# A transformer layer in split fp32: three seven-product units in each up block of the second feed-forward, and longer splits on VectorE

## What is computed

```python
h = rmsnorm(x, ffn2_norm[l])
x = x + 0.5 * swiglu(h, ffn2_w_gate[l], ffn2_w_up[l], ffn2_w_down[l])
...
def swiglu(h, w_gate, w_up, w_down):
    return (jax.nn.silu(h @ w_gate) * (h @ w_up)) @ w_down
```

## Time and profile before

| | |
|---|---|
| median of 3 runs | 1926.8 us (1924.58 to 1927.35) |
| the profiled execution, its own time | 1926.48 us |
| its span, first to last instruction | 1924.7 us |
| granted clock of TensorE | 1.000 |
| PE busy | 1914.1 us (99%), 8998 matmuls |
| DVE busy | 1247.9 us (65%), 1460 instructions |
| ACT busy | 971.4 us (50%), 1232 instructions |
| DMA | 362.51 MB, mean 188 GB/s |
| the blocks (second feed-forward) | from about 1274 us to the end |

### The profile page before, as it was taken

The page is one execution under the profiler, slowest core; times in us unless marked ns, Lnnn a source line. Parts: engine busy times, 40 slices in busy tenths (PEclk is TensorE's granted clock), DMA queues, the critical chain, the costliest instruction groups (busy, mean ns, idle before and its releaser), DMA issues.

```text
span 1924.7 us, 22367 instructions
## 1 busy us (share of the span) xinstructions
PE 1914.1 (99%) x8998; PEld 1608.3 (84%) x8998; DVE 1247.9 (65%) x1460; ACT 971.4 (50%) x1232; POOL 94.6 (5%) x98
## 2 busy tenths in 40 slices
PE   9999999999999999999999999999999999999999
PEld 7788888888889888988888888888888888888987
DVE  5545445545445455575567765688877988788786
ACT  6544435444444445455466664565555555555553
POOL 0000000000000001221332001000000000000000
PEclk9999999999999999999999999999999999999999
DMA  9755555555555555445443555455555656555554
GB/s 331 257 194 192 182 194 194 190 190 192 196 166 201 186 191 187 153 156 193 151 139 127 194 178 174 150 180 181 193 195 175 220 207 224 180 189 184 190 193 163
DMA packets 179433, 362.51 MB, mean 188 GB/s; under 512 B 7041, under 2 KB 18305, under 8 KB 178689
## 3 DMA queue, kind: packets, MB, share of 16 engines
q1 hardware_dynamic: 179040, 360.88, 55.1%
q10 hardware_dynamic: 288, 0.19, 0.0%
HBM read 358.95 MB, written 2.10 MB: 188 GB/s over the span
## 4 chain that ended last, share of the span: by engine, by line
PE 96%; DMA 1%; POOL 1%; ACT 1%; DVE 0%; issue 0%; SPq 0%; DVEq 0%; ACTq 0%; POOLq 0%
PE acc L1935 19%; PE acc L1937 19%; PE acc L1936 19%; PE acc L1946 10%; PE acc L1948 10%; PE acc L1947 10%; PE tr L1904 2%; PE small L2167 2%; DMA w_raw<-in_ffn_w_gate 1%; PE small L1948 1%; PE small L1946 1%; PE small L1947 1%; PE tr L1961 0%; PE tr L1948 0%; PE tr L1946 0%; PE tr L1947 0%
## 5 line engine op out<-in xcount | busy, mean ns | idle before, releaser
L736 ACT ACTIVATE w_hi<-w_raw 128x1024 fp32r<-128x1024 f32 (+2 forms) x616 | 619.1, 1033 | 431.9 <-PE acc L1937 304.9
L1226 DVE TENSOR_TENSOR w_lo<-w_raw,w_hi 128x1024 fp32r<-128x1024 f32 (+3 forms) x432 | 509.7, 1210 | 303.3 <-ACT w_hi L736 301.0
L1935 PE MATMUL acc<-w_hi,hT_hi 128*128 128x512 f32 (+2 forms) x1120 | 433.2, 387 | 3.7 <-DVE w_lo L1226 3.7
L1937 PE MATMUL acc<-w_lo,hT_hi 128*128 128x512 f32 (+2 forms) x1120 | 430.1, 384 | 0.0
L1936 PE MATMUL acc<-w_hi,hT_lo 128*128 128x512 f32 (+2 forms) x1120 | 429.7, 384 | 0.0
L1293 DVE TENSOR_TENSOR w_lo<-w_raw,w_hi 128x1024 fp32r<-128x1024 f32 (+2 forms) x320 | 344.3, 1126 | 40.8 <-ACT w_hi L736 22.4
L1935 PEld LDWEIGHTS acc<-w_hi,hT_hi 128*128 128x128 f32 x1120 | 210.4, 188 | 43.7 <-issue 4.9
L1937 PEld LDWEIGHTS acc<-w_lo,hT_hi 128*128 128x128 f32 x1120 | 210.2, 188 | 40.5
L1936 PEld LDWEIGHTS acc<-w_hi,hT_lo 128*128 128x128 f32 x1120 | 210.4, 188 | 39.0
L1946 PE MATMUL acc<-w_hi,hT_hi 128*128 128x512 f32 (+1 forms) x520 | 200.4, 385 | 0.0
L1948 PE MATMUL acc<-w_lo,hT_hi 128*128 128x512 f32 (+1 forms) x520 | 199.6, 384 | 0.0
(11 more groups left out here) (312 smaller groups left out, 2189.7 us busy)
## 6 DMA issues: line engine op xcount, KB each, us to landing
w_raw<-in_ffn_w_down SPq DMA_DIRECT2D x74, 1024.0 KB, 5.0
w_raw<-in_ffn_w_up SPq DMA_DIRECT2D x71, 1024.0 KB, 5.1
w_raw<-in_ffn_w_gate SPq DMA_DIRECT2D x69, 1024.0 KB, 5.0
w_raw<-in_w_in SPq DMA_DIRECT2D x36, 1024.0 KB, 5.1
w_raw<-in_w_out SPq DMA_DIRECT2D x16, 1024.0 KB, 5.0
w_raw<-in_ffn_w_down SPq DMA_DIRECT2D x16, 768.0 KB, 4.4
w_raw<-in_ffn_w_gate SPq DMA_DIRECT2D x20, 512.0 KB, 4.0
w_raw<-in_ffn_w_up SPq DMA_DIRECT2D x18, 512.0 KB, 4.9
```

Source lines behind the costliest of these rows:

```text
L736: nc.scalar.activation(piece(w_hi, c % SPLIT, k0, k1, width), piece(raw, c % RAW, k0, k1, width), ACT.Copy).then_inc(hi_done, 1)
L1226: v.tensor_tensor(piece(w_lo, c % RAW, k0, k1, width), piece(raw, c % RAW, k0, k1, width), piece(w_hi, c % SPLIT, k0, k1, width).bitcast(F ...
L1935: mm(dst, xh, wh, start=first and kk == 0, stop=False)
L1937: ins = mm(dst, xh, wl, start=False, stop=last and kk == tiles - 1)
```

## The change

Each up block has units at rows 0, 2 and 4, and for each side plain slots of four, three and three tiles. The first half's down blocks have three units for four, with five plain slots a side (4, 4, 4, 3, 3). The second half's down blocks keep their shape. A third `hS` sum is made (`H_SUMS` 3), out of a third `flat`, for which ACT copies two more tiles in `flat_x`; `A_SUMS` becomes (3, 3).

DVE's splits of plain slots and raw slots are one operation each for the whole slot (`lo_whole`, `lo_raw`), where there were two; those of made slots stay two. A raw slot lies in another order: its middle two tiles hold the first side's two row tiles, the outer two the second side's; the tile that is used only in combinations is tile 0, so that the other three are contiguous. Down units are loaded with two DMAs of 512 KB for one of 1024 KB, as up units were. The sign of one token sum and the operands of the first combination are turned, the first combination now reading one tile twice (a broadcast operand).

```diff
-PLAIN_PARTS = {n: halves(n) for n in range(2, 5)}
-RAW_PARTS = ((0, 1), (2, 4))
+RAW_PARTS = ((1, 2), (2, 4))
 MADE_PARTS = ((0, 2), (2, 4))
...
-                DUOS.append(Duo(True, h, b, min(4, tiles - 4 * b) * P, [0, 2], [(4, 4), (8, 4), (12, 4)]))
+                DUOS.append(Duo(True, h, b, min(4, tiles - 4 * b) * P, [0, 2, 4], [(6, 4), (10, 3), (13, 3)]))
             for j in range(DB // 2):
-                DUOS.append(Duo(False, h, j, NW, *(([0, 2, 4, 6], [(8, 4), (12, 4), (16, 4), (20, 4)]),
+                DUOS.append(Duo(False, h, j, NW, *(([0, 2, 4], [(6, 4), (10, 4), (14, 4), (18, 3), (21, 3)]),
                                                    ([0, 2, 4], [(6, 4), (10, 3), (13, 3), (16, 3)]))[h]))
...
-                fetches[r], fetches[r + 1] = 2 if duo.up else 1, 0
+                fetches[r], fetches[r + 1] = 2, 0
...
-        H_SUMS, A_SUMS = 2, (4, 3)
+        H_SUMS, A_SUMS = 3, (3, 3)
...
+                        sp.dma_start(tiles[:, 1:3, 0:d.width], rows_of(wl, k0, 2, slice(n0, n0 + d.width))).then_inc(loaded[c % RAW], 16)
+                        sp.dma_start(tiles[:, 0:4:3, 0:d.width], rows_of(wr, k0, 2, slice(n1, n1 + d.width))).then_inc(loaded[c % RAW], 16)
...
             def flat_x():
 
-                for b in range(2):
-                    act.wait_ge(tr_ready[b], groups["x_o"] + 1)
+                for n in range(H_SUMS):
+                    act.wait_ge(tr_ready[n % 2], groups["x_o"] + n // 2 + 1)
                     for m in range(2):
-                        k = 2 * b + m
-                        nc.scalar.activation(flat[b][:, m, :], tr[:, b, m * SEQ:(m + 1) * SEQ], ACT.Copy,
+                        k = 2 * n + m
+                        nc.scalar.activation(flat[n][:, m, :], tr[:, n % 2, m * SEQ:(m + 1) * SEQ], ACT.Copy,
                                              scale=gains[:, col["ffn2_norm"] + k:col["ffn2_norm"] + k + 1])
+                    if n % 2:
+                        turned_hi(hT_hi, 4 * (n // 2), groups["x_o"] + n // 2, 0, gain=col["ffn2_norm"])
+                        hi(slots["w_o"] + 3, 0, 4, NW)
...
-                v.tensor_tensor(made[:, 0:2, :], b[:, 1:4:2, :], b[:, 0:2, :], ALU.subtract).then_inc(ev("combined"), 1)
+                v.tensor_tensor(made[:, 0:2, :], b[:, 0:1, :].broadcast_to([P, 2, width]), b[:, 1:4:2, :], ALU.subtract).then_inc(ev("combined"), 1)
...
-            def lo_parts(c, parts, width, unit=None):
-
-                for i, (k0, k1) in enumerate(parts):
-                    if unit is not None and i == 1:
-                        dve.wait_ge(ev("combined"), 2 * unit + 2)
+            def lo_whole(c, k0, k1, width):
+
+                dve.wait_ge(hi_done, 2 * c + 2)
+                v.tensor_tensor(piece(w_lo, c % RAW, k0, k1, width), piece(raw, c % RAW, k0, k1, width),
+                                piece(w_hi, c % SPLIT, k0, k1, width).bitcast(F32), ALU.subtract).then_inc(lo_done, 2)
+
+            def lo_raw(c, n, width):
+
+                dve.wait_ge(ev("combined"), 2 * n + 2)
+                lo_whole(c, 1, 4, width)
+
+            def lo_made(c, width):
+
+                for i, (k0, k1) in enumerate(MADE_PARTS):
...
-                product(P1, *A11, c, 0, w, first, last).then_inc(slot_used, 1)
+                product(P1, *A11, c, 1, w, first, last).then_inc(slot_used, 1)
```

More of the change, by code:

```diff
@@ L253, in layer @@
         xoT_lo = at("xoT_lo", A0 + 44, [P, XH, SEQ], F32R)
[L254 to L260, removed]
+        hS_hi = at("hS_hi", A0 + 48, [P, 3, 4, P], F32R)
+        hS_lo = at("hS_lo", A0 + 54, [P, 3, 4, P], F32R)
+        hS_sum = at("hS_sum", A0 + 54, [P, 3, 4, P])
+        aS_hi = at("aS_hi", A0 + 60, [P, 3, 4, P], F32R)
+        aS_lo = at("aS_lo", A0 + 66, [P, 3, 4, P], F32R)
+        aS_sum = at("aS_sum", A0 + 66, [P, 3, 4, P])
+        flat = [at("flat_0", A0 + 72, [P, 2, SEQ]), flat_1, at("flat_2", A0 + 60, [P, 2, SEQ])]
         memk_nat = at("memk_nat", A0 + 48, [P, MT, XH * P])
@@ L488, in load_unit @@
                         sp.wait_ge(slot_used, 2 * (c - RAW + 1))
+                        tiles = raw[:, c % RAW, :].rearrange("p (k n) -> p k n", k=4)
                         if d.up:
[L490 to L493, removed]
-                        else:
-                            dst = raw[:, c % RAW, :].rearrange("p (k n) -> p k n", k=2)
-                            sp.dma_start(dst, rows_of(wd, f0 + k, 2, slice(2 * d.block * NW, 2 * (d.block + 1) * NW))).then_inc(loaded[c % RAW], 16)
+                            n0 = n1 = (f0 + 4 * d.block) * P
+                            k0, wl, wr = k, wg, wu
+                        else:
+                            n0, n1 = 2 * d.block * NW, (2 * d.block + 1) * NW
+                            k0, wl, wr = f0 + k, wd, wd
+                        sp.dma_start(tiles[:, 1:3, 0:d.width], rows_of(wl, k0, 2, slice(n0, n0 + d.width))).then_inc(loaded[c % RAW], 16)
+                        sp.dma_start(tiles[:, 0:4:3, 0:d.width], rows_of(wr, k0, 2, slice(n1, n1 + d.width))).then_inc(loaded[c % RAW], 16)
                     def load_plain(c, side, k, tiles):
@@ L1206, in _ @@
             flat_x()
-            turned_hi(hT_hi, 0, groups["x_o"], 0, gain=col["ffn2_norm"])
-            hi(slots["w_o"] + 3, 0, 4, NW)
             turned_hi(hT_hi, 4, groups["x_o"] + 1, 0, gain=col["ffn2_norm"])
@@ L1264, in token_sums @@
                 done(v.tensor_tensor(dst[:, 0, :], src[:, 0, P:SEQ], src[:, 1, P:SEQ], ALU.add))
-                done(v.tensor_tensor(dst[:, 2, :], src[:, 0, 0:P], src[:, 0, P:SEQ], ALU.subtract))
+                done(v.tensor_tensor(dst[:, 2, :], src[:, 0, P:SEQ], src[:, 0, 0:P], ALU.subtract))
                 done.wait()
@@ L1364, in duos @@
                 combine(DUOS[0].raws[0], 0, NW)
-                lo_parts(DUOS[0].raws[0], RAW_PARTS, NW, 0)
-                lo_parts(DUOS[0].raws[0] + 1, MADE_PARTS, NW)
+                lo_raw(DUOS[0].raws[0], 0, NW)
+                lo_made(DUOS[0].raws[0] + 1, NW)
                 for m, d in enumerate(DUOS):
@@ L1383, in duos @@
                             combine(d.raws[n], u0 + n, w)
-                            lo_parts(d.raws[n], RAW_PARTS, w, u0 + n)
+                            lo_raw(d.raws[n], u0 + n, w)
                             if n == 1 and turns_in(d):
                                 turn_round_lo(m, 0)
-                            lo_parts(d.raws[n] + 1, MADE_PARTS, w)
-                        lo_parts(d.firsts[n], PLAIN_PARTS[tiles], w)
+                            lo_made(d.raws[n] + 1, w)
+                        lo_whole(d.firsts[n], 0, tiles, w)
                         if n == 0 and m and DUOS[m - 1].up:
@@ L1399, in duos @@
                             take_first(m)
-                        lo_parts(d.seconds[n], PLAIN_PARTS[tiles], w)
+                        lo_whole(d.seconds[n], 0, tiles, w)
                         if n == 0 and u1 == len(d.plains):
@@ L1407, in duos @@
                             token_sums(aS_sum[:, n], flat[n % 2])
-                        lo_parts(e.raws[0], RAW_PARTS, e.width, u0 + u1)
+                        lo_raw(e.raws[0], u0 + u1, e.width)
                         for n in new_sums(m):
                             sums_lo(aS_lo[:, n], aS_sum[:, n], aS_hi[:, n], sums_number(m, n))
-                        lo_parts(e.raws[0] + 1, MADE_PARTS, e.width)
+                        lo_made(e.raws[0] + 1, e.width)
             def ffn(f, name):
```

## The result

The changed kernel takes **1930.61 us** in the median of 14 runs (1928.07 to 1932.84), the kernel before 1926.22 us in the same sessions (14 runs). The ratio is 1.0023, 95% interval 1.0016 to 1.0031: slower by 4.4 us, where +0.8 us was forecast. It lies in the range (1923 to 1931.5), and just past the 0.2% from which the prediction calls it slower, to which it gave 0.12; the interval begins at 0.16%, so that side of the line isn't certain. The profiled execution took 1931.74 us, its span is 1929.9 us.

The account below looks back on a forecast made before the run. PE's matmul list bounds the kernel, with VectorE having two tenths or less of its time free; -5.3 us of matmuls and +6.1 of stalls make +0.8 on 1926.48, so 1927.6 us, range 1923 to 1931.5.

Parts of the forecast that it names:

- PE's list: TensorE's matmuls in the second feed-forward: 24 of 8998 fewer, net -5.3 us; a block of 42.45 us for 43.13.
- DVE's list: VectorE's work from one take_second to the next in an up block with two token sums: 41.8 us, before 37.8.
- rival 3: Long splits cost as much as their parts, 1.4 us more a block: 1934 us; chance 0.13 in milder and full forms.
- rival 1: Joining splits frees the whole fixed 0.15 us, 0.8 us less VectorE work a block: 1924.6 us; chance 0.10.
- The new wait: PE waits 2.0 us for take_second before a block's third product, twice, behind blocks with two token sums; 2.1 each with restart.
- the two behind: Starts of the blocks after the two long waits, with one token sum: 0.3 + 0.11 us of stall each.
- The narrow block: The 384-wide block, near the edge for VectorE: a stall of 1.1 us in two pieces.
- Take_parts and the loads: Take_parts moved behind the first second-side split, and down units' loads in two issues: both to cost nothing.
- what a wait costs: Price of each long PE wait at a block's start: 2.0 us, plus 0.11 for a first start of 0.34, not 0.227.
- 0.227 us apart still: Sign that the prediction holds: the distance between starts of PE's 512-wide matmuls stays unchanged.
- a dearer broadcast operand: The combining operation's broadcast read costs more than the 1.22 us taken: at most 0.16 x 3 a block, +2 us.
- Rival 2: PE never waits because VectorE's list fits after all, so the whole 5.3 us come: 1921.5 us; chance 0.07.

Follow-up runs that it names:

- four of seven waits of 1.92 us: Kernel before, with operations that change nothing holding VectorE up so that PE waits 1.91 to 1.93 us at seven places; 1947.15 us.
- 0 of 7 behind 1.66 us: Kernel before, with VectorE held up so that PE waits 1.64 to 1.67 us at seven places; 1940.67 us.
- the two of this length with split halves: Two long waits of the changed kernel with its splits in two operations again, three units kept; 1927.49 us, ratio 1.0005 to the kernel before.
- the wait of 2.97 us: Longest wait in the kernel before with VectorE held up ahead of take_second in seven up blocks for seven different lengths; 1938.25 us.
- the kernel with seven long waits: Kernel before, with VectorE held up so that PE waits 2.39 to 2.41 us at seven places; 1954.42 us.

## Why the prediction was right on the waits and short on their price

- **PE's list.** -5.3 us for 24 matmuls, a block of 42.45 us: blocks without sums were 42.44 and 42.45 us long, and once DVE's lateness is gone the kernel is 5.0 us faster than before. Right.
- **DVE's list.** Counted 1.75 and 2.28 us for the long splits and 1.22 for the combination with its broadcast operand; measured:

```profile
L1291 DVE TENSOR_TENSOR w_lo<-w_raw,w_hi 128x1536 fp32r<-128x1536 f32 x96 | 168.5, 1756 | 42.8 <-ACT w_hi L736 36.9 <-ACT w_hi L811 3.0
...
L1291 DVE TENSOR_TENSOR w_lo<-w_raw,w_hi 128x2048 fp32r<-128x2048 f32 x34 | 77.8, 2290 | 13.3 <-ACT w_hi L736 13.0 <-ACT w_hi L811 0.3
L1282 DVE TENSOR_TENSOR w_raw<-w_raw 128x1024 f32<-128x1024 f32 x38 | 46.3, 1219 | 0.0
```

  1.756, 2.290 and 1.219 us. The wait for the last high part is 2.35 us for 2.3. So rival 3 (long operations as dear as their parts) falls, and rival 1 (joining frees the whole fixed part) too: a row of splits still overlaps by 0.085 us (2.35 us for two at 1318.05), and the waits were not shorter than counted.
- **The new wait.** Place, releaser and length as told: PE starts 2.08 us late for 2.0 at the second up block of the first half and the third of the second, and 0.41 for 0.3 at the two behind (by the profile's count 1.92 and 0.25 us). The narrow block was given 1.1 us in two pieces. It has two: 0.84 us and a restart of 0.11 at its end, and the 0.38 us at its third unit, where the prediction saw its smallest margin, 0.4 us in a 512-wide block. Together 1.33 us, less 3 x 0.173 for its matmuls, make 0.81 of the 0.83 us by which that stage is longer. Take_parts and the loads made no wait. In all the waits cost about 6.7 us where 6.1 were taken.
- **The step that failed: what a wait costs.** "PE waits 2.0 us, and 0.11 more since its first start after a wait is 0.34 instead of 0.227 ...". That price was read from a wait of 0.20 us, the only one before. Behind a wait ten times as long stand two terms: the restart of 0.11 us, and with it 1.6 us at half the clock. Twice 1.6 us is 3.2, a term that the sum did not have: -5.3 + 6.7 + 3.2 = 4.6 us, where the profiled execution shows 4.8 without the 0.45 us ahead of the blocks, and the medians 4.4. The prediction put PE's matmuls "0.227 us apart still" among its signs, and this one was wrong. The Trainium skill, TensorE: Matmul & The Clock Gate, in its section on how the clock's oscillation bites in real kernels, describes a kernel in which PE waits some 3 to 5 us for loads between tiles and begins each next tile at the slow clock. The trace agrees in kind, at 0.50 behind each of the two waits, but these were shorter, 1.92 us, and what was measured decides.
- **The range** held the time by luck. Its upper end, 1931.5 us, was set for a dearer broadcast operand and the start of rival 3, and neither came; a fall of the clock was in no rival. Four of the 14 executions lie above 1931.5.
- **Rival 2** (PE never waits, 1921.5 us) was wrong for this change. It is what the kernel gives when ACT's order is turned (1921.23).

What stays open: why four of seven waits of 1.92 us were followed by a fall and three were not. The changed kernel's runs have granted clocks of 0.998 (five, median 1932.14 us) and 0.999 (nine, 1930.15 us); that the latter had one fall for two would fit, but only one execution has a trace, and 0.999 also stands at six of 26 executions of the kernel before, which has no long wait.

## What to carry to other kernels

When an engine's list is shortened, first add up the list of the engine that feeds it, block by block with its forced waits: 41.8 us of work in a block of 42.45 looked like a fit, and was not, for 3 us of waits in it that nothing filled. A fixed wait in the feeding engine is the first place to look: one step moved on ACT made of +4.4 us a gain of 5.0. And an idle time of TensorE of about 2 us had here a second price, 1.6 us, that those of 1.7 us and less did not have; matmuls of no use in the gap took that price away.

## What the runs showed of the hardware that was not expected

- The granted clock can fall from 2.4 to 1.2 GHz behind a wait of 1.9 us in an otherwise full list of matmuls: 0 of 7 behind 1.66 us (and none behind the two of this length with split halves), 4 of 7 behind 1.92 in one kernel and 2 of 2 in another, 6 of 7 behind 2.40. Each fall makes seven or eight 512-wide starts 0.43 us apart, 1.4 to 1.6 us.
- In the changed kernel the slow distances begin two starts after the wait's end (0.33 and 0.23 us come first); behind the wait of 2.97 us they begin with it, and in the kernel with seven long waits one to seven starts later.
- Nine matmuls of no use in a gap of nine starts did not delay the next product, and in two such gaps saved 2.8 us.
- VectorE's fp32 split is linear up to 2048 columns (0.685, 1.219, 1.756, 2.290 us), and with a broadcast operand no dearer (1.219 us, 1024 columns).
